# Attention scores with the keys on the partitions, reduced by GpSimd, in a fused layer kernel

## The reference, cut to what matters

```python
q = q.reshape(b_, nc, CHUNK, N_KV_HEADS, GROUP, HEAD_DIM)      # 16 chunks, 2 kv heads, 8 query heads each
kb = make_band(k...); vb = make_band(v...)                     # 128 keys: previous chunk, own chunk
logits = einsum('bnqkgd,bnskd->bnkgqs', q, kb) / sqrt(HEAD_DIM) + band_bias(rel_bias)
logits = where(valid, logits, NEG)                             # chunk 0 has no previous chunk
m = maximum(max(logits, axis=-1), sink)                        # a learned sink for each head
p = exp(logits - m)
denom = sum(p, axis=-1) + exp(sink - m)
o = einsum('bnkgqs,bnskd->bnqkgd', p / denom, vb)
mixed = concat([o * silu(g_attn), conv * silu(g_conv)])
```

## Time and profile before

| | |
|---|---|
| median of 3 runs | 1341.59 us (1341.4 to 1342.21) |
| the profiled execution | 1342.15 us, its span 1340.4 us |
| TensorE matmul busy | 1327.5 us (99%) |
| VectorE busy | 908.1 us (68%) |
| ScalarE busy | 543.5 us (41%) |
| GpSimd busy | 90.3 us (7%) |
| granted TensorE clock | 0.998 of full |

### The profile page before, as it was taken

One profiled execution on the slowest core, in us unless ns is written; L12 is line 12 of the kernel. 1 busy time (PEld: TensorE's weight loads), 2 busy tenths in 40 slices (PEclk: granted clock), 3 DMA queues, 4 the chain that ended last, 5 costly groups with the idle time before them and its releaser, 6 DMA issues.

```text
span 1340.4 us, 16528 instructions
## 1 busy us (share of the span) xinstructions
PE 1327.5 (99%) x6038; PEld 1099.2 (82%) x6038; DVE 908.1 (68%) x1132; ACT 543.5 (41%) x946; POOL 90.3 (7%) x151
## 2 busy tenths in 40 slices
PE   9999999999999999999999999999999999999997
PEld 8887888888888888888888888888888888888886
DVE  6899766323577449975589745997439896665376
ACT  7856532232233433434334333334323444321444
POOL 1222220000000000000000000000001121100001
PEclk9999999999999999999999999999999999999999
DMA  9779995988797998779987799787898978899768
GB/s 368 288 271 373 389 351 150 319 310 318 290 297 241 308 301 277 230 219 317 302 287 249 235 312 305 225 261 244 295 348 296 326 259 287 298 306 360 267 260 301
DMA packets 167888, 390.01 MB, mean 291 GB/s; under 512 B 77920, under 2 KB 90240, under 8 KB 146176
## 3 DMA queue, kind: packets, MB, share of 16 engines
q1 hardware_dynamic: 148272, 322.08, 71.7%
q0 software_dynamic: 18240, 62.92, 12.8%
q10 hardware_dynamic: 1296, 3.96, 0.8%
HBM read 294.18 MB, written 98.93 MB: 293 GB/s over the span
## 4 chain that ended last, share of the span: by engine, by line
PE 91%; DVE 6%; issue 2%; DMA 1%; ACT 0%; POOL 0%; POOLq 0%; DVEq 0%; ACTq 0%
PE banks L2009 86%; PE banks L2038 1%; PE banks L2050 1%; DVE x_main L1357 1%; DVE w_ring L1344 1%; DMA x_park<-e 1%; PE banks L1969 1%; PE banks L2059 1%; PE banks L2060 1%; DVE raw L1454 0%; PE banks L1994 0%; DVE raw L1442 0%; DVE e L1502 0%; DVE raw L1436 0%; DVE z L1466 0%
## 5 line engine op out<-in xcount | busy, mean ns | idle before, releaser
L2009 PE MATMUL banks<-x_main,w_ring 128*128 128x512 f32 x2352 | 551.0, 391 | 1.0 <-DVE e L1505 0.5
L2009 PEld LDWEIGHTS banks<-x_main,w_ring 128*128 128x128 f32 x2352 | 438.5, 188 | 91.9 <-issue 1.4
L970 ACT ACTIVATE w_ring<-raw 128x1024 fp32r<-128x1024 f32 x223 | 235.5, 1056 | 544.4 <-PE banks L2009 537.6
L1344 DVE TENSOR_TENSOR w_ring<-raw,w_ring 128x1024 fp32r<-128x1024 f32 x223 | 272.9, 1224 | 218.3 <-ACT w_ring L970 216.7
L2009 PE MATMUL banks<-x_far,w_ring 128*128 128x512 f32 x1680 | 393.4, 391 | 0.1
L2009 PEld LDWEIGHTS banks<-x_far,w_ring 128*128 128x128 f32 x1680 | 313.0, 188 | 64.7 <-DVE e L1502 0.5
L2009 PE MATMUL banks<-w_ring,x_main 128*128 128x512 f32 (+1 forms) x1020 | 230.9, 387 | 0.3 <-DVE e L1502 0.3
L2009 PEld LDWEIGHTS banks<-w_ring,x_main 128*128 128x128 f32 x1020 | 189.9, 188 | 39.6 <-DVE e L1502 0.7
L505 POOL DMA_DIRECT2D x_park<-x_main x104 | 56.1, 539 | 1006.0 <-DVE x_main L1357 1005.9
L1001 ACT ACTIVATE x_main<-z 128x512 fp32r<-128x512 f32 x104 | 64.9, 624 | 116.6 <-issue 81.5
L1357 DVE TENSOR_TENSOR x_main<-z,x_main 128x512 fp32r<-128x512 f32 x104 | 71.3, 687 | 37.7 <-ACT x_main L1001 37.5
(11 more groups left out here) (164 smaller groups left out, 845.3 us busy)
## 6 DMA issues: line engine op xcount, KB each, us to landing
x_far<-x_park SPq DMA_DIRECT2D x84, 1024.0 KB, 6.3
x_main<-x_park SPq DMA_DIRECT2D x84, 1024.0 KB, 6.1
raw<-in_w_blocks_dram SPq DMA_DIRECT2D x127, 512.0 KB, 5.4
x_park<-x_main POOLq DMA_DIRECT2D x104, 512.0 KB, 5.7
q_cur<-qkv_park SPq DMA_DIRECT2D x64, 128.0 KB, 4.9
z<-mix_park SPq DMA_DIRECT2D x16, 512.0 KB, 7.7
z<-in_x_dram SPq DMA_DIRECT2D x6, 1024.0 KB, 13.0
x_park<-e POOLq DMA_DIRECT2D x8, 512.0 KB, 6.4
```

What stands on the lines that cost most here:

```text
L970: act.activation(w_ring[:, n % NW, :, 0, :], raw[:, c, k:k + 2, :], ACT.Copy).then_inc(w_hi_ready, 1)
L1344: dve.tensor_tensor(w_ring[:, n % NW, :, 1, :], raw[:, c, k:k + 2, :], w_ring[:, n % NW, :, 0, :], ALU.subtract).then_inc(w_lo_ready, 1)
L2009: op = pe.matmul(bank, left, right, start=(first and i == 0), stop=(kt == HK - 1 and i == 2), skip_group_check=goes_on)
```

## The change

The keys go on the partitions. The scores of a unit are made with the keys as the stationary operand, two matmuls of 128x512 into one bank, keys on the 128 partitions, 8 heads x 64 queries along the row. The bias is stored in that layout. Maximum and sum over the keys are then over the partitions: two `partition_all_reduce` on GpSimd of 128x512 each, queued at o = 1 and o = 5. The sink is a second half of the row, so that subtraction and exponential run over 128x1024 in one operation each. The probabilities aren't normalised; instead the gate is multiplied with the reciprocal of the sum, which VectorE takes on blocks of 32 that it turns before and back after (`weight_gate`, o = 11). The transposes of the probabilities are gone, and both splits of them read SBUF. The value transpose is at o = 0, its split at o = 2 and 3; the shift is at o = 4, the exponential at o = 5, the splits at o = 6 and 7.

```diff
-            def turn_probs(u):
-                pe.wait_ge(logits_read, 2 * u + 2)
...
-                for j in range(PAIRS):
-                    op = pe.transpose(pt_ps[:, j * P:(j + 1) * P], probs[:, j, 0:BAND], ident[:, :])
-                op.then_inc(probs_turned, 1)
+                queries = q_cur[:, :, :].rearrange("p h s -> p (h s)")
+                pe.matmul(logit_ps, k_cur[:, 0, :], queries, start=True, stop=False)
+                pe.matmul(logit_ps, k_cur[:, 1, :], queries, start=False, stop=True).then_inc(qk_done, 1)
...
+            def key_max(u):
+                pool.wait_ge(logits_read, u + 1)
+                if u > 0:
+                    pool.wait_ge(shift_step, 2 * u)
+                pool.partition_all_reduce(top, logits[u % 2][:, 0, :], P, bass.bass_isa.ReduceOp.max).then_inc(max_ready, 1)
+
+            def key_sum(u):
+                pool.wait_ge(exp_done, u + 1)
+                if u > 0:
+                    pool.wait_ge(weight_step, 6 * u)
+                pool.partition_all_reduce(total, probs[:, 0, :], P, bass.bass_isa.ReduceOp.add).then_inc(key_sum_ready, 1)
...
             def exp_logits(u):
...
+                act.wait_ge(shift_step, 2 * u + 2)
+                act.activation(probs[:, :, :], probs[:, :, :], ACT.Exp).then_inc(exp_done, 1)
...
-            def turn_p(u):
-                act.wait_ge(probs_turned, u + 1)
-                act.activation(pt_hi[:, :], pt_ps, ACT.Copy).then_inc(pt_hi_ready, 1)
+            def split_p(u):
+                act.wait_ge(exp_done, u + 1)
+                if u > 0:
+                    act.wait_ge(pv_done, u)
+                act.activation(pt_hi[:, :], probs[:, 0, :], ACT.Copy).then_inc(pt_hi_ready, 1)
...
+                dve.scalar_tensor_tensor(out=logits[kv][rows, 0, :], in0=logit_ps[rows, :], scalar=SCALE,
+                                         in1=bias[rows, kv * PAIRS * 2:(kv + 1) * PAIRS * 2, :].rearrange("p h s -> p (h s)"),
                                          op0=ALU.mult, op1=ALU.add).then_inc(logits_read, 1)
...
+            def shift_logits(u):
+                kv = u % 2
+                if u == 0:
+                    dve.wait_ge(edges_written, 2 * KVH)
+                dve.wait_ge(max_ready, u + 1)
+                dve.tensor_tensor(top, top, logits[kv][:, 1, :], ALU.max).then_inc(shift_step, 1)
+                dve.wait_ge(shift_step, 2 * u + 1)
                 if u > 0:
...
+                    dve.wait_ge(key_sum_ready, u)
+                    dve.wait_ge(weight_step, 6 * u)
+                    dve.wait_ge(pt_lo_ready, u)
+                dve.tensor_tensor(probs[:, :, :], logits[kv][:, :, :], top.unsqueeze(1).to_broadcast([P, 2, N]), ALU.subtract
+                                  ).then_inc(shift_step, 1)
+
+            def weight_gate(u):
+
+                dve.wait_ge(key_sum_ready, u + 1)
+                dve.tensor_tensor(total, total, probs[:, 1, :], ALU.add).then_inc(weight_step, 1)
+                dve.wait_ge(weight_step, 6 * u + 1)
+                dve.transpose(total_turned, total).then_inc(weight_step, 1)
+                dve.wait_ge(weight_step, 6 * u + 2)
+                dve.reciprocal(inv_turned, total_turned.rearrange("p (c t) -> p c t", t=32)[:, :, 0]).then_inc(weight_step, 1)
+                dve.wait_ge(weight_step, 6 * u + 3)
+                for par in range(2):
+                    rows = slice(par * HEAD, (par + 1) * HEAD)
+                    mine = inv_turned.rearrange("p (j a c) -> p a j c", a=2, c=2)[rows, par, :, :]
+                    dve.transpose(inv_row[rows, :].rearrange("p (j c t) -> p j c t", j=PAIRS, c=2),
+                                  mine.unsqueeze(3).to_broadcast([HEAD, PAIRS, 2, 32])).then_inc(weight_step, 1)
+                dve.wait_ge(weight_step, 6 * u + 5)
+                dve.wait_ge(g_loaded, u * 16 + 16)
+                dve.tensor_tensor(g_cur[:, :, :], g_cur[:, :, :], inv_row.rearrange("p (j k) -> p j k", j=PAIRS), ALU.mult
+                                  ).then_inc(weight_step, 1)
...
-                dve.tensor_tensor(pt_lo[:, :], pt_ps, pt_hi[:, :], ALU.subtract).then_inc(pt_lo_ready, 1)
+                dve.tensor_tensor(pt_lo[:, :], probs[:, 0, :], pt_hi[:, :], ALU.subtract).then_inc(pt_lo_ready, 1)
...
                         if o == 1:
+                            scale_logits(u)
+                        elif o == 3 and u % 2 == 0:
+                            turn_v_lo(u // 2)
+                        elif o == 4:
                             shift_logits(u)
...
+                        elif o == 7:
+                            split_p_lo(u)
+                        elif o == 11:
+                            weight_gate(u)
...
-                    if quarter == 2 and late_w:
-                        w_lo(n + 2)
                     if quarter == 1:
-                        if W_TABLED <= n + 2 < STEPS and not late_w:
+                        if W_TABLED <= n + 2 < STEPS:
                             w_lo(n + 2)
```

More of the change, by code:

```diff
@@ L31 @@
 REL = 192
-LB = BAND + 1
 N = 512
@@ L312, in build @@
         zeros = sb("zeros", [P, CHUNK], X + 18 * KB + 1600)
[L314 to L325, removed]
+        bias = sb("bias", [P, HEADS, CHUNK], Z)
+        logits = [sb(f"logits{i}", [P, 2, N], Z + 4096 + 4096 * i) for i in range(KVH)]
+        probs = sb("probs", [P, 2, N], Z + 12288)
+        top = sb("top", [P, N], Z + 16384)
+        total = sb("total", [P, N], Z + 18432)
+        total_turned = probs[:, 1, :]
+        inv_turned = small[:, 104:120]
+        inv_row = total[:, 0:PAIRS * CHUNK]
+        v_win = sb("v_win", [P, BAND], Z + 20480)
+        g_cur = sb("g_cur", [P, PAIRS, CHUNK], Z + 20992)
+        o_mix = sb("o_mix", [P, PAIRS, CHUNK], Z + 22016)
+        o_lo = sb("o_lo", [P, PAIRS, CHUNK], Z + 23040)
+        q_cur = sb("q_cur", [P, PAIRS * 2, CHUNK], Z + 24064, F32R)
+        k_cur = sb("k_cur", [P, 2, BAND], Z + 26112, F32R)
+        pt_hi = sb("pt_hi", [P, N], Z + 27136, F32R)
+        pt_lo = sb("pt_lo", [P, N], Z + 29184, F32R)
+        v_cur = sb("v_cur", [P, KVH, 2, HEAD], Z + 31232, F32R)
         u_buf = sb("u_buf", [P, 2, 2 + S], Z + 32 * KB - 32)
@@ L922, in _ @@
                         store_park(PARK_AT[n, quarter])
+                    u, o = unit_at(n, quarter)
+                    if 0 <= u < UNITS:
+                        if o == 1:
+                            key_max(u)
+                        elif o == 5:
+                            key_sum(u)
                 b, p, q = place(n + 2) if n + 2 < STEPS else (BLOCKS, 0, 0)
@@ L1568, in shift_logits @@
                     dve.wait_ge(bias_loaded, 32)
-                lo = CHUNK if u < 2 else 0
                 if u > 1:
-                    dve.wait_ge(exp_done, u - 1)
-                dve.scalar_tensor_tensor(out=logits[kv][:, :, lo:BAND], in0=logit_ps[:, :, 1, lo:],
-                                         scalar=-SCALE, in1=bias[:, kv * PAIRS:(kv + 1) * PAIRS, lo:],
+                    dve.wait_ge(max_ready, u - 1)
+                rows = slice(CHUNK if u < 2 else 0, P)
+                dve.scalar_tensor_tensor(out=logits[kv][rows, 0, :], in0=logit_ps[rows, :], scalar=SCALE,
+                                         in1=bias[rows, kv * PAIRS * 2:(kv + 1) * PAIRS * 2, :].rearrange("p h s -> p (h s)"),
```

104 lines of the change are left out of this document (34 added, 70 removed).

## The result

The changed kernel takes 1384.77 us (1381.78 to 1385.7, four runs) where the kernel before takes 1341.49 beside it: a ratio of 1.0318, with an interval of 1.03 to 1.0336. It is slower by 43 us. The forecast was slower by 130.

What follows compares the result with a forecast made beforehand. TensorE, 91% of the wait chain, bounds the kernel; VectorE blocked by GpSimd would take over. 1342.15 - 12.3 + 32 x (21.9 - 17.46) = 1472 us; range 1332 to 1850, the mechanism's own 1400 to 1700.

Steps and rivals of the forecast that it cites:

- What bounds the kernel, and slower: Whole kernel: TensorE bounds it before, VectorE held up by GpSimd in the attention after; slower, chance 0.80.
- TensorE gains 12.3 us, floor 1329.8: Attention on TensorE: dropped transposes and wider score products save 0.38 us a unit, leaving at least 1329.8 us.
- VectorE, 2.5 us more a unit: VectorE in the attention: 5.03 us a unit removed, 7.53 in their place, giving 15.7 us of work a unit.
- T = 3.6 for each reduction: GpSimd: one all-reduce of 128x512 assumed as three passes over the columns, 3.6 us; bounds 1.20 and 80.
- 1241 + 64 T: Whole kernel: forecast time in us by the length T of one reduction, never under 1329.8.
- VectorE is blocked for the whole reduction: Attention: VectorE operations with two SBUF inputs wait out each GpSimd reduction; a unit takes 14.7 + 2T, 21.9 us.
- The three overlaps of the earlier trace: Earlier trace: VectorE operations with two SBUF operands end 1.08 to 1.09 us after GpSimd's additions, read as alternating.
- The buffer evens out dense and light units: Weight splits 6.1 us ahead of TensorE: they even out dense and light units, not a mean that is too long.
- A: Attention: the all-reduce doesn't block VectorE, only dense stretches hurt; 1336 us, faster; chance 0.14.
- D: Attention: cover lost alone, VectorE's 2.5 us a unit without any block; 1336 us; no separate chance given.
- three boundaries, 2 us each: Dense stretches at block boundaries, without blocking: 7.5 us short against 6.1 ahead, 6 us in all, giving 1336.
- the longest weight split: VectorE in the attention: weight splits were to show a maximum of 1.22 + T instead of 1.72 us.

Runs made afterwards that it cites:

- (1): The changed kernel with both GpSimd reductions replaced by memsets, all VectorE work kept: 1344.3 us, ratio 1.0021 to the kernel before.
- (3): The changed kernel with memsets for both reductions and VectorE's addition, transposes and reciprocal of the sum left out: 1323.82 us, ratio 0.9866.
- the small program: Separate program, not the layer: GpSimd reductions or plain additions of 128x512, alone and beside 110 VectorE operations of three kinds; alone, maximum 1.78 us, sum 3.23.
- the fast version: The changed kernel with sink subtracted from the bias, sum's inverse as exp(-log) on ScalarE, inverse and gate additions at quarter 2: 1328.07 us, ratio 0.9901.

## Why the prediction was wrong

- *What bounds the kernel, and slower.* Right. TensorE was the bound, VectorE became one, and GpSimd's own latency is hardly waited for (4.4 us).
- *TensorE gains 12.3 us, floor 1329.8.* Too small: 18, floor 1323.8. The steps behind transposes and half-width products shrank as well, and their longer spacing stood in the earlier trace rows (5.48 and 5.56 for 5.44).
- *VectorE, 2.5 us more a unit.* Right: (1) against (3) is 990.9 - 910.9 = 80.0 us, 2.5 a unit. Transposes at 0.71 and 0.44 for the assumed 0.69 and 0.42; reciprocal 0.25 for 0.18.
- *T = 3.6 for each reduction.* 1.78 and 3.23 alone, 2.70 and 3.71 in the kernel: a pair of 6.4 for 7.2, from a bound that spanned 1.2 to 80. But of the 6.4 a part is waiting for the port, in which VectorE is not held; what the forecast's formula asks for is the time alone, a pair of 5.0, T = 2.5. With that alone put right the forecast's 1241 + 64 T says 1401 and not 1472: this term was mis-sized, and it is the largest single part of the miss.
- *VectorE is blocked for the whole reduction, 2T - 1.4 + 0.4 = 6.2 us a unit.* **This step failed.** The measured hold is 1.97 us a unit, and 1.94 where the turns are left out (973.1 - 910.9 = 62.2 us over 32 units). Of the 4.2 us too many 2.2 are the pair's length, 7.2 for 5.0. Of these 5.0 us at most 1.4 + 2.6 = 4.0 hold the port, 1.0 less; and the last 1.0 is put down to where they fall: beside operations on PSUM (the version with the gate's additions first has the maximum there), or begun while VectorE had the port. The three overlaps of the earlier trace rows were plain additions, for which 0.9 of 1.1 is held; from them the forecast took "runs only once GpSimd's is over". The Trainium skill, "SBUF — State Buffer", section "SBUF: two separate sides", calls the lock exclusive for the whole instruction. The small program does not bear that out for this instruction: VectorE got through 21 to 23% of each, between two stops. The forecast also let operations with one SBUF input run beside GpSimd; in the small program they are the ones held up.
- *The buffer evens out dense and light units.* **This failed too**, in the other direction. With the hold as measured, the forecast's own unit is 15.7 + 2.0 = 17.7 us, 0.24 over the floor's 17.46: 1329.8 + 32 x 0.24 = 1337. Measured 1384.8. TensorE's crowded units take 18.9 to 24.7 us, its light ones the floor of 17.2 to 17.6 and never less, so that what a crowded stretch loses stays lost. The slack of a mean unit is no slack in a crowded one, and the slices of VectorE before, with sevens to nines in three places, said where they are.
- *Rivals A and D, 1336.* D, the load alone, is (1): 1344.3. The estimate for three boundaries, 2 us each, was too low: 20.5 over the floor, not 6. A holds in so far as long VectorE operations do lie under a reduction.
- *Not priced:* the lower clock behind TensorE's waits. It is most of the 22.7 us that the products are busy longer, of the 63 us of span over version (3).
- *What it would show:* the longest weight split was to take 1.22 + T = 4.8 us. Two of the 95 in the attention reach 3.27 us, and none of the others is over 1.23. TensorE did wait for VectorE, but above all for the split of the probabilities, 23.0 us of the 40.4 that its products stand in the attention, not for the weight split.

```profile
PE banks L2084 <- DVE pt_lo L1634: 23.0, 10, 6.4
```

So the errors went opposite ways: a block three times too large, in a mean that forgives too much. Put right, the first takes the sum from 1472 to 1337; what is left up to the 1385 that was measured is the second's. That the sign came out right rests on the overload, which was real, and not on the sum: with the right hold the same sum says 1337, faster than before. In that part it was luck.

Open: why the cost above 946 us is 0.5 and not 1. That about half of the extra work falls into units with room fits the slices, but was not tried by moving it.

## What to carry to other kernels

Price added work on a nearly full engine in its most crowded stretch, one stretch at a time, and count there what holds it up as work of its own. Two costs that are each small against the slack are large together once they exceed it. Before handing work to a lighter engine, look at what is queued behind the instruction that will wait: 24 us here hung on the places of a logarithm with its exponential and of two additions.

## What the runs showed of the hardware

- A reduction over partitions of 128x512 takes 1.78 us for a maximum and 3.23 for a sum, far under the 80 us that had been its upper bound.
- Consecutive VectorE operations with two SBUF inputs can keep GpSimd out to their end: for 13 us in the small program (110 operations of 128x64), for 6.3 us once in the fast version (9.51 for 3.23). In the kernel after no reduction waited longer than one operation (at most 1.1 us).
- A VectorE operation with one SBUF input (scalar multiplication in fp32) is held up by GpSimd too: by 0.9 us of a 1.1 us addition, 1.4 of a 1.8 us maximum, 2.6 of a 3.3 us sum, in two pieces for the reductions. Operations reading PSUM are not (14.53 us for 110 beside all three).
- TensorE idle for 3.6 us came back at a mean granted clock of 0.64 for 4.7 us, at 0.384 us a product instead of 0.226.
- A step of 24 products takes 5.56 us right behind transposes of fp32 (four in the kernel before, one in version (3)), 5.48 behind products of 256 columns, and 5.44 behind products of 512.
